# Hybrid decoder trunk: two of each pair's four weight sums made by adding transfers

## The reference

```
h     = rmsnorm(x) * (1 + sc1) + sh1
proj  = h @ w_in                       # q, k, v, gates of two attentions
mixed = sigmoid(ga) * moba(...) + sigmoid(gb) * dsa(...)
x     = x + gt1 * rmsnorm(mixed @ w_out)
h     = rmsnorm(x) * (1 + sc2) + sh2
f     = (silu(h @ w_gate) * (h @ w_up)) @ w_down          # 2816 wide
x     = x + gt2 * rmsnorm(f)
```

## Time and profile before

| | |
|---|---|
| median of 3 runs | 849.33 us (847.21 to 850.21) |
| profiled execution | 848.88 us, its span 847.1 us |
| TensorE busy | 832.3 us, 98% |
| VectorE busy | 690.0 us, 81% |
| ScalarE busy | 458.5 us, 54% |
| GpSimd busy | 121.3 us, 14% |
| DMA mean | 229 GB/s, 194.09 MB |

### The profile page before, as it was taken

One profiled execution on the slowest core, in us unless ns is written; L12 is line 12 of the kernel. 1 busy time (PEld: TensorE's weight loads), 2 busy tenths in 40 slices (PEclk: granted clock), 3 DMA queues, 4 the chain that ended last, 5 costly groups with the idle time before them and its releaser, 6 DMA issues.

```text
span 847.1 us, 11576 instructions
## 1 busy us (share of the span) xinstructions
PE 832.3 (98%) x4131; PEld 689.5 (81%) x4131; DVE 690.0 (81%) x1180; ACT 458.5 (54%) x732; POOL 121.3 (14%) x92
## 2 busy tenths in 40 slices
PE   8999999999999999999999999999999999999897
PEld 5877888888888888888888788888888878778685
DVE  5898889888788776786789899898778878989973
ACT  5665555555657334533575655555575644554442
POOL 5500300302220021120420040040040000000300
PEclk9999999999999999999999999999999999999999
DMA  8996666575418888787428756666542577083431
GB/s 343 402 370 229 222 256 254 199 275 211 150 51 303 295 289 325 240 328 277 171 95 335 261 199 251 246 243 229 199 150 100 222 301 280 17 327 144 179 145 50
DMA packets 34795, 194.09 MB, mean 229 GB/s; under 512 B 4273, under 2 KB 4529, under 8 KB 17714
## 3 DMA queue, kind: packets, MB, share of 16 engines
q1 hardware_dynamic: 33410, 189.64, 60.1%
q0 software_dynamic: 1328, 3.71, 1.2%
HBM read 192.29 MB, written 1.05 MB: 228 GB/s over the span
## 4 chain that ended last, share of the span: by engine, by line
PE 83%; DVE 7%; DMA 5%; issue 2%; ACT 2%; SPq 1%; DVEq 0%; ACTq 0%
PE ps L1735 22%; PE ps L1737 22%; PE ps L1736 22%; PE ps L1848 4%; DMA wide_t<-scale_first 3%; DVE w_lo L1156 3%; DMA raw<-w_stream 2%; ACT w_hi L769 2%; PE ps L1912 2%; PE ps L2154 1%; PE ps L1772 1%; PE ps L1773 1%; PE ps L1779 1%; PE ps L1933 1%; PE ps L1934 1%
## 5 line engine op out<-in xcount | busy, mean ns | idle before, releaser
L1156 DVE TENSOR_TENSOR w_lo<-raw,w_hi 128x2048 fp32r<-128x2048 f32 (+2 forms) x126 | 286.5, 2279 | 57.2 <-ACT w_hi L769 56.1
L1735 PE MATMUL ps<-w_hi,t_hi 128*128 128x512 f32 (+2 forms) x712 | 282.0, 396 | 1.7 <-DVE w_lo L1156 0.9
L1737 PE MATMUL ps<-w_hi,t_lo 128*128 128x512 f32 (+2 forms) x712 | 275.1, 386 | 0.0
L1736 PE MATMUL ps<-w_lo,t_hi 128*128 128x512 f32 (+2 forms) x712 | 274.5, 385 | 0.0
L769 ACT ACTIVATE w_hi<-raw 128x2048 fp32r<-128x2048 f32 (+2 forms) x128 | 240.6, 1883 | 40.6 <-DMA raw<-w_stream 34.4
L666 POOL PARTITION_ALL_REDUCE wide_t<-wide_t x20 | 80.0, 3999 | 556.5 <-DVE wide_t L1282 555.5
L1735 PEld LDWEIGHTS ps<-w_hi,t_hi 128*128 128x128 f32 x712 | 133.8, 188 | 30.3 <-DVE w_lo L1156 2.9
L1737 PEld LDWEIGHTS ps<-w_hi,t_lo 128*128 128x128 f32 x712 | 133.7, 188 | 27.8
L1736 PEld LDWEIGHTS ps<-w_lo,t_hi 128*128 128x128 f32 x712 | 134.0, 188 | 25.2
L1282 DVE SCALAR_TENSOR_TENSOR wide_t<-ada,cs,wide_t 128x1024 f32<-128x1024 f32 x80 | 110.2, 1377 | 2.0 <-DMA ada<-w_ada 1.7
L1735 PE MATMUL ps<-w_hi,m_hi 128*128 128x512 f32 x208 | 84.3, 405 | 0.0
(11 more groups left out here) (257 smaller groups left out, 1078.4 us busy)
## 6 DMA issues: line engine op xcount, KB each, us to landing
raw<-w_stream SPq DMA_DIRECT2D x124, 1024.0 KB, 5.3
ada<-w_ada SPq DMA_DIRECT2D x80, 512.0 KB, 5.7
wide_t<-gains POOLq DMA_DIRECT2D x7, 512.0 KB, 4.8
mixed<-w_stream SPq DMA_DIRECT2D x3, 1024.0 KB, 7.6
raw<-w_stream SPq DMA_DIRECT2D x4, 656.0 KB, 6.9
mixed<-scale_first SPq DMA_DIRECT2D x2, 1024.0 KB, 10.4
wide_t<-shift_first SPq DMA_DIRECT2D x4, 512.0 KB, 11.1
wide_t<-scale_first SPq DMA_DIRECT2D x2, 1024.0 KB, 12.7
```

What stands on the lines that cost most here:

```text
L1156: nc.vector.tensor_tensor(w_lo[:, U % RING, a:n], src[:, a:n], w_hi[:, U % RING, a:n].bitcast(F32), ALU.subtract).then_inc(s_lo, 1)
L1735: nc.tensor.matmul(dst, hi, w_h, start=first, stop=False)
L1736: nc.tensor.matmul(dst, hi, w_l, start=False, stop=False)
L1737: return nc.tensor.matmul(dst, lo, w_h, start=False, stop=last)
```

## The change

Of the four sums of a pair, two are no longer made by VectorE: `w_sum += upper(j)` and `upper(j) += lower(j)`. GpSimd issues for each a transfer from `w_stream` in HBM that adds to what is in SBUF. The first waits for the low part of unit 0, the second for the landing of `upper(j)`; ScalarE waits on their semaphores before it makes the high parts of units 1 and 4. Both pairs' transfers stand in GpSimd's list before the reductions of the last table.

Besides: `add_tokens` is cut in two, part 0 (three operations) in step `sums_step(l) - 1` and part 1 (two) in step `sums_step(l)`; layer 1's pieces per step go from (1, 3, 1, 1, 1, 0, 0, 1, 0, 0, 0) to (2, 2, 3, 0, 0, 0, 0, 0, 1, 0, 0) and its table from step 8 to step 10; in `twin_lo` the third `add_products` goes ahead of a split; and `gated` waits on `s_table`.

```diff
-TWIN_SUMS = (1, 4, 3, 6)
+TWIN_SUMS = (3, 6)
...
-    return (1, 3, 1, 1, 1, 0, 0, 1, 0, 0, 0), (8,)
+    return (2, 2, 3, 0, 0, 0, 0, 0, 1, 0, 0), (10,)
...
+            def add_stored(l, j):
+
+                U = BASE[l] + twin_unit(l, j)
+                upper, landed, count = stored(*SOURCE[U + 4])
+                pool.wait_ge(s_lo, U + 1)
+                pool.dma_start(w_sum, w_stream[l, up_at(j), :, :], accum_op=ALU.add).then_inc(s_first_sum, 16)
+                pool.wait_ge(landed, count)
+                pool.dma_start(upper, w_stream[l, up_at(j) + 1, :, :], accum_op=ALU.add).then_inc(s_upper_sum, 16)
...
+                for j in TWINS[l]:
+                    add_stored(l, j)
                 finish(n + 3, 0, l, 3)
...
-                    act.wait_ge(s_w_sum, 4 * twin_no(layer, name[1]) + TWIN_SUMS.index(name[2]) + 1)
+                    act.wait_ge(s_w_sum, 2 * twin_no(layer, name[1]) + TWIN_SUMS.index(name[2]) + 1)
+                elif name[0] == "twin" and name[2] == 1:
+                    act.wait_ge(s_first_sum, 16 * (twin_no(layer, name[1]) + 1))
+                elif name[0] == "twin" and name[2] == 4:
+                    act.wait_ge(s_upper_sum, 16 * (twin_no(layer, name[1]) + 1))
...
-                if name[0] == "twin" and name[2] == 0:
-                    add_first(U)
-                elif name[0] == "twin" and name[2] == 3:
+                if name[0] == "twin" and name[2] == 3:
                     add_corner(U - 3)
 
-            def add_first(U):
-
-                upper, landed, count = stored(*SOURCE[U + 4])
-                dve.wait_ge(s_lo, U + 1)
-                dve.wait_ge(landed, count)
-                nc.vector.tensor_tensor(w_sum, w_sum, upper, ALU.add).then_inc(s_w_sum, 1)
-
             def add_lower(U):
 
-                upper = stored(*SOURCE[U + 4])[0]
                 lower, landed, count = stored(*SOURCE[U + 5])
                 dve.wait_ge(landed, count)
-                nc.vector.tensor_tensor(upper, upper, lower, ALU.add).then_inc(s_w_sum, 1)
...
-            def add_tokens(l):
+            def add_tokens(l, part):
 
                 upper, lower = slice(0, 4), slice(4, KT)
                 one, two = slice(0, P), slice(P, 2 * P)
+                if part:
+                    link(nc.vector.scalar_tensor_tensor(out=sums[:, upper, one], in0=sums[:, lower, two], scalar=-1.0,
+                                                        in1=sums[:, upper, one], op0=ALU.mult, op1=ALU.subtract))
+                    nc.vector.scalar_tensor_tensor(out=sums[:, lower, one], in0=sums[:, lower, one], scalar=-1.0,
+                                                   in1=sums[:, upper, one], op0=ALU.mult, op1=ALU.subtract).then_inc(s_sums, 1)
+                    return
...
-                link(nc.vector.scalar_tensor_tensor(out=sums[:, upper, one], in0=sums[:, lower, two], scalar=-1.0,
-                                                    in1=sums[:, upper, one], op0=ALU.mult, op1=ALU.subtract))
-                nc.vector.scalar_tensor_tensor(out=sums[:, lower, one], in0=sums[:, lower, one], scalar=-1.0,
-                                               in1=sums[:, upper, one], op0=ALU.mult, op1=ALU.subtract).then_inc(s_sums, 1)
...
+                add_products(l, j, twin_b, twin_b, OUT, 4, 3)
                 split_lo(l, behind[2])
-                add_products(l, j, twin_b, twin_b, OUT, 4, 3)
...
                 dve.wait_ge(s_sq, squares(n, 0))
+                dve.wait_ge(s_table, 4 * l + (1 if mid else 3))
                 gate_part(l, t, 0, 512)
...
                         if t == 0 and j == sums_step(l):
-                            add_tokens(l)
+                            add_tokens(l, 1)
+                        elif t == 0 and j == sums_step(l) - 1:
+                            add_tokens(l, 0)
```

More of the change, by code:

```diff
@@ L418, in hybrid_decoder_trunk @@
         s_w_sum = sem("twin_blocks_weights_added")
+        s_first_sum = sem("twin_blocks_first_sum_landed")
+        s_upper_sum = sem("twin_blocks_upper_sum_landed")
         s_kept = sem("twin_blocks_first_product_copied")
```

## The result

The changed kernel takes 859.36 us (median of 4 runs, 858.02 to 860.17), the kernel before in the same session 848.27 us (4 runs, 847.16 to 850.21): a ratio of 1.0124 [1.0109, 1.014]. I forecast slower, by about 5 us; it is 11. The time lies inside the range of 846.5 to 860.0, by 0.6 us. The profiled execution took 860.17 us with a span of 858.4, against 848.88 and 847.1.

The account below looks back on a forecast made before the run. TensorE, busy 98% of the span, was taken to bound the kernel. The terms: 848.9 - 0.7 - 4.3 - 1.1 + 5.4 + 1.0 - 0.6 + 2.65 + 2.1 = 853.4 us, range 846.5 to 860.

Parts of the forecast that it names:

- Third copy: First pair: the third copy of products ahead of a split removes TensorE's wait at product 6; -0.7 us.
- Pieces and table: Second pair: reductions moved beside step 10 remove TensorE's 2.7 us wait and 1.6 us of low clock; -4.3 us.
- rival (d): End of layer 1: reductions come too late, final table after 834; 855 to 857 us, chance 0.04.
- Step 2: Layer 1: only two short token-sum operations stay between the gates, so TensorE's wait goes; -1.1 us.
- Step 1: Layer 1: token-sum part 0 between two gate products makes TensorE stand 3.8 us, plus 1.6 for the clock; +5.4 us.
- Rival (c): Step 1's wait is absent because VectorE reaches the gate 3 us earlier; 843.2 to 845 us, chance 0.10.
- Layer 0: Token-sum part 0 also runs in its last step beside GpSimd's reduction, delaying the border; +1.0 us (0.4 to 2).
- The length L: Steps 4 and 7: unit 0's low part to first transfer's landing, 7.2 us; waits L - 4.55, L - 5.1.
- No clock price for these waits: Steps 4 and 7: waits of 2.65 and 2.1 us, just under 2.69, bring no lower clock; 0 us.
- rival (b): Steps 4 and 7: transfer much slower, L from 9 us, waits 4.5 and 3.9 plus clock; 860.2 us, chance 0.12.
- The likeliest case "alone": Whole kernel: L 5.8 to 9 us with both new VectorE waits paid; 850.5 to 858 us, chance 0.57.
- The second transfer of a pair at 0: Both pairs: it lands some 5 us after the first and is wanted 15 us later; 0 us.

Follow-up runs that it names:

- the kernel without waits: Changed kernel with all four sums on VectorE and token-sum part 0 behind step 1's second gate, layer 1 only: 842.5 us; with the third copy back behind the split 841.59.
- The three kernels without waits: Changed kernel, token-sum part 0 behind the second gate, layer 1 only: second transfer kept 842.54 us; all sums on VectorE 842.5; that with third copy put back 841.59.

## Why the prediction was right in direction and wrong in size

- *Third copy.* The 0.7 us of the first pair went, but the kernel with the pieces alone had no wait for `pj` either. The right number stood on the wrong edit, which is luck. The copy's own share stays open: a loss of 0.3 us a pair in the kernel without waits, and a gain of 0.9 in the first pair beside the pieces alone. Both medians are lower without the move, by 2.0 and 0.9 us, but the intervals of the ratios overlap.
- *Pieces and table.* Booked -4.3, and the second pair gave -4.25: the wait of 2.69 us and the 1.6 us of low clock behind it are gone. At the end the table was made from 845.30 to 846.52, just ahead of the border at 846.68, as worked out from the earlier trace rows: rival (d) didn't come.
- *Step 2.* Booked -1.1, measured -1.25: right, the wait of 1.06 us is gone.
- *Step 1.* Booked 3.8 + 1.6, measured 3.67 + 1.6 = 5.4 with the rest of the step. Rival (c) is out. But the 1.6 holds for this profile only (last section).
- *Layer 0.* The step that I took for 1.0 cost 2.0. I had multiplied by 1.7 as in the earlier trace rows. The large operation took 3.35 us instead of 2.28 (1.5 times), but the small one in place, 0.69 us without the reduction, took 2.62, and all three ended at 421.1 instead of 420.5. The split of 1312 columns took 2.25 where I had 1.5; that was misread, since the same split already took 2.56 us in the kernel before. VectorE's timeline before (first row) and after:

```profile
417.87 2.56 DVE L1156 TENSOR_TENSOR w_lo<-raw,w_hi 128x1312 fp32r<-128x1312 f32 x1 [3.28 <-ACT w_hi L769]
...
414.42 3.35 DVE L1201 TENSOR_TENSOR token_sums<-t_hi,t_lo 128x2048 f32<-128x2048 f32 x1
417.80 2.62 DVE L1202 TENSOR_TENSOR token_sums<-token_sums 128x512 f32<-128x512 f32 x1
420.45 0.69 DVE L1203 TENSOR_TENSOR token_sums<-token_sums 128x512 f32<-128x512 f32 x1
421.18 2.25 DVE L1173 TENSOR_TENSOR w_lo<-raw,w_hi 128x1312 fp32r<-128x1312 f32 x1
```

- *The length L.* Booked 7.2 = 2.8 fixed + 4.4 for the data; measured 8.2 and 9.5. The fixed part was right: 7.8 - 4.9 = 2.9 us. The data part was 0.5 too short (4.9 us), and I had left out the 0.4 us from the end of the low part (724.8) to the issue (725.18). In step 7 SyncE issued loads of the pair's own blocks at 773.20 and 775.40, and the DMA engines still moved 410 GB/s from 778 to 780, behind the transfer's issue at 777.87. The transfer landed after 9.1 us instead of 7.8 (7.9 to 8.6 in the other kernels with both), and the load of 775.40 after 6.7 instead of 4.9, most likely since they met there. My sentence that no load of SyncE is out at this time was false there. The way behind the landing held: 7.15 us booked from the start of the high part to the turn, 740.16 - 732.99 = 7.17 and 794.14 - 786.98 = 7.16 measured. The room that TensorE has was 0.5 us larger each time than my 4.55 and 5.1 (8.2 - 3.2 = 5.0, 9.5 - 3.85 = 5.65), which took 1.0 us off L's 3.3. What remains is +2.3 us: idle of 3.2 + 3.85 us instead of 2.65 + 2.1.
- *No clock price for these waits.* This is the step that failed most. "They are just under 2.69" was a margin of 0.04 us on an estimate of L with bounds from 5 to 10. Measured: 1.4 + 1.65 = 3.1 us. The waits turned out longer in sum, but each single one was shorter than 2.69 (1.08 and 2.10, 1.75 and 2.10), and the clock fell all the same. 2.69 us was one wait behind which the clock had fallen, and I used it as the shortest that can do so; the table in the last section has a fall behind 1.78 us, and none behind 3.64.
- *The sum of the misses*: layer 0 1.0, L 2.3, clock 3.1, and 0.4 in all the rest: 6.8 us, which is 860.2 - 853.4. The second pair met rival (b)'s condition, L from 9 us on, and the whole came out at (b)'s 860.2, for which I had 0.12. That agreement is partly luck: (b) has 8.4 us of waits and 1.0 for layer 0 where 7.0 and 2.0 were measured, and the two transfers of a pair weren't mixed, as (b) had it. The likeliest case "alone" ended at 858.
- The second transfer of a pair at 0: right. GpSimd's queue: the reductions at the end started at 830.82, no later than their last piece.

## What to carry to other kernels

A sum of 2.3 us on VectorE became a transfer of 8 us with a wait for its start, so it should only be moved where its result is wanted later than the whole transfer takes: the second of each pair was free there, and gained nothing, as VectorE wasn't the bound. Work on VectorE between two results that TensorE takes one after the other cost nearly its full length (3.67 of 3.77 us), though the same work one instruction later was free; ask of each moved step which of the two places it has. Where a wait of 2 us or more is expected, book the clock both ways, and put its price into the centre: behind the ten pairs of such waits in these profiles the clock fell eight times. Before taking a duration from a quiet stretch, look for the same instruction at the same place in the trace.

## What the runs showed of the hardware that I had not expected

- *The price of one idle stretch is not fixed.* All idles of TensorE of 0.3 us or more in layer 0's last step and layer 1's FFN, over the 14 profiles:

  | idle of TensorE | how often | lower clock in it or behind it |
  |---|---|---|
  | single, 0.48 to 1.71 us | 9 | 0 |
  | single, 1.78 us (layer 0) | 5 | 2 |
  | single, 2.69 us (second pair before) | 1 | 1 |
  | 0.58 to 1.75 us, two small matmuls, 2.1 us | 10 | 8 |
  | single, 3.64 to 3.67 us (step 1) | 6 | 5 |

  The same 3.64 to 3.67 us of idle in step 1 was followed by the full clock in one profile (window 686 to 688: 1.00), by 1.6 us of loss in the changed kernel, and by a lower clock from 682 to past 688 with part 0 left out of layer 0. The windows of that kernel, between its turn of tile 0 and the end of the slow part:

```profile
682.00:684.00 2.00, 0.62 (x3) 0.63 (x4) 1.93 (x4) 0.00 (x0) 0.00 (x0) 0.50 0.97 383
684.00:686.00 2.00, 2.00 (x7) 1.52 (x5) 2.00 (x2) 1.90 (x2) 0.00 (x0) 0.50 0.57 229
686.00:688.00 2.00, 2.00 (x6) 1.62 (x5) 2.00 (x4) 0.28 (x1) 0.00 (x0) 0.50 0.24 57
```

  Time and clock go together run by run: of the 10 runs with the sums on VectorE the fastest (847.4 us) had a mean granted clock of 0.998, the slowest three (851.5 to 852.0) 0.993; with both transfers and the token sums late, 850.7 us at 0.996 and 855.1 at 0.991. The three kernels without waits spread over only 0.3 to 1.8 us, at 0.998 to 1.0.
- *Behind two idles with two small matmuls between them the clock mostly fell.* 1.08 and 2.10 us brought the clock to 0.50, and so did seven more of the ten such pairs; 1.22 and 2.10, and 0.58 and 2.10, did not. No profile has a single idle of 2.1 us, so what the first of the two adds isn't shown.
- *Beside a reduction on GpSimd the slowdown of VectorE is not one factor*: 1.3 to 1.85 times for operations of 128x2048 that began beside it (2.96 to 4.21 us instead of 2.28), 3.8 times for one of 128x512 in place (2.62 against 0.69 us, the same in the kernel with all sums on VectorE). In that kernel a split at 817.79, begun just before the reductions at 817.97, took its usual 2.28 us, and the two reductions 8.53 us instead of 7.48.
- *An adding transfer keeps all DMA engines busy at half the rate* (213 against 424 GB/s), and its issue takes GpSimd 0.85 to 1.2 us against 0.53 to 0.55 for a plain one.
